# DMA transposes for more tiles, an earlier query block and constant products in front of the value projection

## The reference

```
h = RMSNorm(x) * (1 + scale1) + shift1
q, f, i, g, B, C, hv = h @ W_in                    # 7 blocks of 512 columns
HGRN2 (4 heads of 128): f_t = lb + (1-lb) sigmoid(f);  S_t = diag(f_t) S_{t-1} + (1-f_t) outer i_t
       o_t = S_t^T q_t, RMSNorm per head, times g_onorm * silu(g)
conv:  y = B * causal_conv3(C * hv)
x = x + gate1 * (concat[o, y] @ W_out)
x = x + gate2 * (relu((RMSNorm(x) * (1+scale2) + shift2) @ W_up)^2 @ W_down)
out = RMSNorm(x) * g_final
```

## Time and profile before

| what | value |
|---|---|
| median of 3 runs | 861.19 us (858.78 to 865.7) |
| the profiled execution, its own time | 858.85 us |
| its span on the slowest core (the others: 854.6 to 856.6) | 857.3 us |
| PE busy | 810.3 us, 95% of the span |
| DVE, ACT, POOL busy | 454.1, 369.2, 173.1 us |
| mean granted TensorE clock | 0.991 of full speed |
| HBM traffic | 123.93 MB read, 22.68 MB written |

### The profile page before, as it was taken

One profiled execution on the slowest core, in us unless ns is written; L12 is line 12 of the kernel. 1 busy time (PEld: TensorE's weight loads), 2 busy tenths in 40 slices (PEclk: granted clock), 3 DMA queues, 4 the chain that ended last, 5 costly groups with the idle time before them and its releaser, 6 DMA issues.

```text
span 857.3 us, 16496 instructions; the slowest of 8 cores (854.6 to 857.3 us)
## 1 busy us (share of the span) xinstructions
PE 810.3 (95%) x5917; PEld 512.2 (60%) x5917; DVE 454.1 (53%) x876; ACT 369.2 (43%) x803; POOL 173.1 (20%) x231
## 2 busy tenths in 40 slices
PE   1479999999999999999999999999999999999996
PEld 1348876586876868656545654564456445644864
DVE  2366997377777867953015553455345535541522
ACT  3267963364676778447303322332233213310412
POOL 3110143353324231510003011101110111111002
PEclk9989999999999999999999999999999999999998
DMA  8999935988893349599995325212421432112001
GB/s 151 191 193 189 198 99 95 209 208 175 197 222 129 125 146 153 149 174 192 188 198 184 112 56 160 99 50 62 151 96 50 78 107 75 38 37 99 26 1 50
DMA packets 38957, 109.57 MB, mean 128 GB/s; under 512 B 15030, under 2 KB 16054, under 8 KB 33884
## 3 DMA queue, kind: packets, MB, share of 16 engines
q0 software_dynamic: 6624, 44.14, 31.1%
q1 hardware_dynamic: 30524, 58.34, 22.1%
q10 hardware_dynamic: 1728, 6.03, 2.2%
HBM read 123.93 MB, written 22.68 MB: 171 GB/s over the span
## 4 chain that ended last, share of the span: by engine, by line
PE 83%; DMA 11%; DVE 2%; issue 2%; ACT 1%; POOL 1%; DVEq 0%; ACTq 0%; POOLq 0%; SPq 0%
PE B L510 82%; DMA gates<-xr 4%; DMA win<-w_in 3%; DMA xe<-xp 3%; PE B L521 1%; ACT W L537 1%; DMA xn<-xp 1%; DMA xr<-xs 1%; POOL xr L544 0%; DVE Sd L544 0%; POOL mix L544 0%; DVE W L554 0%; DVE sg L554 0%; DVE ub L544 0%; DVE W L544 0%
## 5 line engine op out<-in xcount | busy, mean ns | idle before, releaser
L510 PE MATMUL B<-h2T,wup 128*128 128x384 bf16 (+1 forms) x1536 | 240.2, 317 | 0.0
L510 PE MATMUL B<-wdn,uT 128*128 128x512 bf16 (+1 forms) x1120 | 235.9, 373 | 0.0
L510 PE MATMUL B<-hT,win 128*128 128x256 bf16 (+1 forms) x1728 | 194.3, 269 | 6.1 <-DMA win<-w_in 5.4
L510 PEld LDWEIGHTS B<-h2T,wup 128*128 128x128 bf16 x1536 | 149.5, 98 | 83.8
L537 ACT ACTIVATE W<-B 128x384 f32<-128x384 f32 (+2 forms) x209 | 103.6, 497 | 204.3 <-PE B L510 187.3
L510 PEld LDWEIGHTS B<-wdn,uT 128*128 128x128 bf16 x1120 | 109.6, 98 | 124.8
L510 PEld LDWEIGHTS B<-hT,win 128*128 128x128 bf16 x1728 | 158.9, 99 | 27.9 <-issue 7.1
L544 POOL TENSOR_TENSOR xr<-xr,W 128x512 f32<-128x512 f32 x63 | 82.3, 1312 | 291.8 <-DVE W L544 256.3
L544 DVE TENSOR_TENSOR uT<-W,B 128x384 bf16<-128x384 f32 (+1 forms) x160 | 83.8, 525 | 80.5 <-ACT W L537 74.8
L544 DVE TENSOR_TENSOR W<-B,Gp 128x512 f32<-128x512 f32 (+1 forms) x65 | 44.2, 680 | 152.9 <-PE B L510 152.7
L537 ACT ACTIVATE W<-xr 128x1024 bf16<-128x1024 f32 (+2 forms) x19 | 18.3, 965 | 131.5 <-POOL xr L544 126.8
(11 more groups left out here) (157 smaller groups left out, 660.9 us busy)
## 6 DMA issues: line engine op xcount, KB each, us to landing
x<-xr SPq DMA_DIRECT2D x17, 512.0 KB, 10.6
xn<-x SPq DMA_DIRECT2D x17, 512.0 KB, 5.8
xr<-x SPq DMA_DIRECT2D x17, 512.0 KB, 4.1
ada<-w_ada POOLq DMA_DIRECT2D x8, 1024.0 KB, 14.7
xr<-xp SPq DMA_DIRECT2D x16, 512.0 KB, 10.0
wup<-w_up POOLq DMA_DIRECT2D x8, 1024.0 KB, 13.7
wdn<-w_down POOLq DMA_DIRECT2D x8, 1024.0 KB, 39.7
yp<-xr SPq DMA_DIRECT2D x15, 512.0 KB, 2.6
```

Of the source, the lines that this page charges most:

```text
L510: ins = e.matmul(o_, lhsT=l_, rhs=r_, start=st, stop=sp_, skip_group_check=True)
```

## The change

Five things change.

1. `sample_mod` no longer transposes on PE. It issues a DMA transpose (`turn`) into its destination and works in place from there. It is used for S in the mixer and in group 1 of the channel mixer.
2. `norm1` takes DMA transposes for P4 to P7: two of them a tile, and eight DVE operations of 256 columns in place.
3. `norm2` takes its `cross` branch for the first two groups too.
4. win0's load is put ahead of P2's `norm1`, and so ahead of the fetch of P2's tokens.
5. Before the first tiles' steps, 14 operations of two matmuls each are recorded: the identity and mask constants times the identity, 384 columns, into a bank of a new class Z. Nothing reads the result. Their priority is the lowest of all, and the planner may start them from 43,000 ns of its clock on.

A DMA's semaphore now goes by the part of the buffer too, so that the two transposes of one tile count apart.

```diff
@@ Prog
-    CAPS = {"G": (2, 4), ...}
+    CAPS = {"Z": (0, 1), "G": (2, 4), ...}
@@ op
+        o.start = 0.0
...
-            key = eng + ((":in:" + writes[0][0].name) if (...) else (":out:" + reads[0][0].name))
+            key = eng + ((":in:" + writes[0][0].name + writes[0][1]) if (...) else (":out:" + reads[0][0].name))
@@ schedule
-            o.est = 0.0
+            o.est = o.start
@@ sample_mod
-        M, Mn = NR.take()
-        Mb = M[:, :].bitcast(BF16)
-        tr([(Mb[:, j * 128:(j + 1) * 128], nbv[:, j * 128:(j + 1) * 128], ident) for j in range(8)], [nbn, "cB"], [Mn])
+        turn(dst[:, :, c0:c0 + 128], nbv, [nbn], [dst_n + "#d0"], 128 * 2048)
...
-            tt("dve", tmv, trv, scb, ALU.mult, [Mn, "modT%d#%d" % (j_sc // 8, jh)], [Wn])
-            tt("dve", hv, tmv, shb, ALU.add, [Wn, "modT%d#%d" % (j_sh // 8, jh)], ["%s#%d" % (dst_n, jh)])
+            tt("dve", tmv, hv, scb, ALU.mult, [dst_n + "#d0", "modT%d#%d" % (j_sc // 8, jh)], [Wn])
+            tt("dve", hv, tmv, shb, ALU.add, [Wn, dst_n + "#d0", "modT%d#%d" % (j_sh // 8, jh)], ["%s#%d" % (dst_n, jh)])
@@ norm1
+        if ti >= 4:
+            for b in range(2):
+                turn(h[:, :, b * 128:(b + 1) * 128], nbs[b][0], [nbs[b][1]], ["%s#d%d" % (hn, b)], 128 * 2048)
+            for jj in range(8):
+                ts("dve", h[:, jj, :], h[:, jj, :], modT[:, 8 + jj, 0:1], modT[:, jj, 0:1], ALU.mult, ALU.add,
+                   [hn + "#d0", hn + "#d1", "modT0#%d" % (jj // 4), "modT1#%d" % (jj // 4)], ["%s#%d" % (hn, jj)])
+            return h, hn
@@ norm2, branch cross
-                turn(dst, nbv, [nbn], [hn], 128 * 2048)
+                turn(dst, nbv, [nbn], [hn + "#d0"], 128 * 2048)
...
-                       ["%s#%d" % (hn, j), "modT2#%d" % (j // 4), "modT3#%d" % (j // 4)], ["%s#%d" % (hn, j)])
+                       [hn + "#d0", "modT2#%d" % (j // 4), "modT3#%d" % (j // 4)], ["%s#%d" % (hn, j)])
@@ the program's order
+    bank, bn = ZB.take()
+    for i in range(14):
+        mm([(bank[:, 0:384], ident, cB[:, 0:384], True, True) for _ in range(2)], ["cB"], [bn], prio=1e6 + i)
+        P.ops[-1].start = 43000.0
...
+    load_in(0)
     hs[2] = norm1(*tiles[2], eng="pool")
-    for j in (0, 3, 5, 6, 4):
+    for j in (3, 5, 6, 4):
         load_in(j)
...
-                norm2(bgroups[0][n_ - 5:n_ - 4], None, "h2T0_", n_ - 5)
+                norm2(bgroups[0][n_ - 5:n_ - 4], None, "h2T0_", n_ - 5, cross=True)
...
-            norm2(bgroups[1], h2T, "h2T", 0, got)
+            norm2(bgroups[1], h2T, "h2T", 0, got, cross=True)
```

More of the change, by code:

```diff
@@ L60 @@
     BANKS = ["B%d" % i for i in range(8)]
-    CAPS = {"G": (2, 4), "M": (1, 2), "N": (0, 1), "U": (2, 3), "O": (1, 2), "D": (0, 1), "P": (0, 2), "X": (0, 8), "Y": (0, 1)}
+    CAPS = {"Z": (0, 1), "G": (2, 4), "M": (1, 2), "N": (0, 1), "U": (2, 3), "O": (1, 2), "D": (0, 1), "P": (0, 2), "X": (0, 8), "Y": (0, 1)}
     FIFO = "PXUN"
@@ L146, in op @@
         if dma is not None:
-            key = eng + ((":in:" + writes[0][0].name) if (writes and (writes[0][0].rng is not None or not reads)) else (":out:" + reads[0][0].name))
+            key = eng + ((":in:" + writes[0][0].name + writes[0][1]) if (writes and (writes[0][0].rng is not None or not reads)) else (":out:" + reads[0][0].name))
             o.chan = key
@@ L740, in take @@
             return PSB[plan[0][k] if plan else "B0"], n
-    GA, MR, NR, UR, OR, DR, PR, GB, YB = (Banks(c) for c in "GMNUODPXY")
+    GA, MR, NR, UR, OR, DR, PR, GB, YB, ZB = (Banks(c) for c in "GMNUODPXYZ")
     MB2 = 1024 * 512 * 4
@@ L879, in sample_mod @@
     def sample_mod(nbv, nbn, dst, dst_n, c0, j_sh, j_sc, spare=None):
-        M, Mn = NR.take()
-        Mb = M[:, :].bitcast(BF16)
-        tr([(Mb[:, j * 128:(j + 1) * 128], nbv[:, j * 128:(j + 1) * 128], ident) for j in range(8)], [nbn, "cB"], [Mn])
+        turn(dst[:, :, c0:c0 + 128], nbv, [nbn], [dst_n + "#d0"], 128 * 2048)
         for jh in range(2):
             W, Wn = (spare[0][:, jh * 512:(jh + 1) * 512], "%s#%d" % (spare[1], jh)) if spare else WT.take()
-            trv = Mb[:, jh * 512:(jh + 1) * 512].rearrange("p (j s t) -> p j s t", s=16, t=8)
             tmv = W[:].rearrange("p (j s t) -> p j s t", s=16, t=8)
```

## The result

The changed kernel takes **894.23 us** (median of 4 runs, 891.59 to 899.69) against 861.8 us for the kernel before on the same chip (median of 4): a ratio of **1.0369, 95% interval 1.0319 to 1.0419**. It is 3.7% slower; the forecast was 853.4 us.

What follows compares the result with a forecast made beforehand. PE's unbroken work after 62.8 us and when it begins bound the kernel; 858.85 - 6.75 (transposes) - 1.0 (start) = 851.1 us, plus 2.34 to the median of runs gives 853.4 us, range 847 to 861.

Steps and rivals of the forecast that it cites:

- So the waits count 0: Mixer and first two channel-mixer groups: DMA transposes land before PE first reads their tokens, so PE's added wait is 0.
- that of DVE's scaling for the landing: The one added wait named for the DMA transposes: DVE's scaling waits for the landing, 3.2 us quiet, 22.5 us taken.
- 22.5 us: Landing time taken for a DMA transpose under load, from SP's transfers between 219 and 257 us.
- the bound of 47 us at one piece a turn: High end for a transpose beside POOL's loads: 64 pieces an engine, 0.73 us a turn, 47 us.
- the 7.75 us forecast: Total gain on PE's path: 6.75 us from transposes leaving PE plus 1.0 us at the start.
- the 11.3 us that I gave P7: Mixer, tile P7: margin from normalised (300.6 us) to first read (311.95 us), without POOL loads; 7.5 us needed.
- The transposes' price: Mixer and first two channel-mixer groups: 15 batches of 8 transposes leave PE at 0.45 us each, 6.75 us gained.
- The start: Before 70 us: win0 ahead of P2's tokens and constant matmuls gain 1.0 us, between 2.9 gained and 2.5 lost.
- Rival A: Mixer: the planner's new order doubles PE's waits or the constants lose 2.5 us, 856 to 859 us; chance 0.20.
- Rival B: Second channel-mixer group: third block waits for a shared normalised buffer, PE stands 18 us, 871 us; chance 0.11.
- Rival C: All 120 moved transposes: each cost PE its duration, 216 ns, so 26 us go and time is 834 us; chance 0.02.
- the 0.66: Whole kernel: chance given to the forecast's own case, 850 to 857 us around 853.4 us.

Runs made afterwards that it cites:

- experiment 12: Changed kernel with P4, P5, the second group and the first group's sample block back on PE, two up-weight loads a tile later, old start: ratio 1.0001 to the kernel before.
- experiment 8: Kernel before with only the changed kernel's start (query block ahead of the tokens, constants), all transposes on PE: ratio 0.9984.
- experiment 4: Kernel before with only the second channel-mixer group's three blocks transposed by DMA: 884.82 us, ratio 1.0305.
- Experiments 5: Changed kernel with P4's transposes back on PE and a third normalise buffer taken from the evacuation's: 903.8 us, ratio 1.0526 to the kernel before.
- experiment 6: Changed kernel with every DMA transpose replaced by a plain copy of the same 1,024 pieces of 256 bytes: 868.9 us, ratio 1.0126 to the kernel before.
- experiment 10: Changed kernel with P4, P5 and the second group back on PE, and the first two up-weight loads a tile later: ratio 1.0045 to the kernel before.

## Why the prediction was wrong

- **The step that failed** is "So the waits count 0". It compared each landing with PE's first read of the transposed tokens and found 34 us for P5 (P4, S and P6 were given the same lead without working it out). I named the added wait, "that of DVE's scaling for the landing", and not what is queued behind it on DVE; and I did not ask who wants the buffer back that the transpose reads. The waits were not 0: ACT stood 24.05 us for the buffer and DVE 28.10 us for the landing, and PE 15.75 us behind them and 11.14 us just before. On core 4 these two deadlines were 219.3 us (DVE, 247.42 - 28.10) and 212.0 us (ACT, 221.84 - 9.80), with another tile's work behind each. I had named the two buffers, but for the second group alone.
- **The landing was mis-sized.** I took 22.5 us for a transpose under load; P4 had 12.4 to 49.6, the second group's first block 62.3 to 68.4. For P4 22.5 us lies within what six of the cores show (12.4 to 31.7), but cores 4 and 7 reached 49.6 and 40.6. For the second group the bound of 47 us at one piece a turn was the better reading, and still too low: 64 pieces an engine in 66 us are 1.03 us a turn, where the plain transfers of the earlier trace rows had 0.73. The Trainium skill, page "DMA: Bandwidth & Descriptors", section "Queues, rings and completion order", gave 3 to 5 us by my estimate from its rule of whole packets; the second group's 62 to 68 us disagree, for transposes and for plain copies of 256 bytes alike.
- **Where no long wait came, the sum was right in direction and too large.** Cores 0 and 3 have spans of 853.8 and 851.8 us, where both took 856.6 before: 2.8 and 4.8 us of the 7.75 us forecast. P6 and P7 landed within 7.2 us, inside the 11.3 us that I gave P7.
- **The transposes' price** of 0.45 us a batch is in PE's work: from the first `up` matmul to `down` core 3 takes 409.13 - 359.47 - 0.99 (a wait) = 48.67 us, where the kernel before took 416.47 - 366.63 = 49.84 us (366.63 is its first `up` matmul in the view of the earlier trace rows): 0.39 us for each of three batches. But PE's sum alone does not set the slowest core's end: experiment 12 shows no gain from seven batches.
- **The start** agrees with the forecast: values in 7.07 us, queries at 58.8 us on core 3 (60.8 in experiment 8; forecast 61), 1.4 us gained of 1.0 forecast, with no gain inside the interval.
- **Rival A** was too small. **Rival B** had its link right in kind, the shared buffer, and its chain wrong: it gave the first and the third block 48.2 us each, and the first took 62.3 to 68.4 us and the third, with the loads through, 7.7 to 10.3. What counts is ACT's order: of the 18 us that it gave PE the changed kernel shows 1.28, experiment 4 25.8. It forecast slower, 871 us; the 894 us came from another place. **Rival C** is out.
- **Two slips in the prediction's sums** change nothing in the account: with the start's 2.9 us gained the case begins at 858.85 - 6.75 - 2.9 + 2.34 = 851.5 us, not 850, and of the 0.66 it gives 0.34 to the side below 852.6 while its words put a little more above.
- That the transposes would slow the loads was in no rival. Experiments 5 and 6 show it; why the engines move half as much while they do is open, beyond that the time goes within the transposes' packets. It happened at 195 to 270 us and not at the mixer's end, where the second group's stretch moved 178 GB/s on core 4 both with transposes and with plain copies.

## What to carry to other kernels

When a transfer takes over an engine's work, ask two things of each place where it will run: what else is in the queues in that very window, and who wants its source buffer back, on which in-order engine, with what behind it. Ask the same of the first instruction that waits for the result. A margin against the last reader says nothing about these two. A transfer that is harmless in the stretch where one can see it (3.2 us) may take twenty times as long in another; move it only into stretches shown to be quiet, and check again after any load is moved, as experiment 10 shows.

## What the runs showed of the hardware that I had not expected

DMA transposes and POOL's loads can jam each other: on core 4 a transpose of 256 KB took 49.6 us and the load beside it 44.2 us, at 99 GB/s in all, where plain copies of the same pieces left 194 GB/s and 11 us. In these traces the late landings had two or more loads beside them. The jam differed between cores that run the same program at the same time (12.4 to 26.9 us for the same transpose).

The issue of a DMA transpose can hold SP for most of the transfer, with all that SP is to issue next. At the second group on core 0 the issues took 14.97 us of a landing of 62.8 and 39.51 us of one of 45.2, against 1.26 us when quiet:

```profile
365.22 14.97 SPq L571 DMA_TRANSPOSE h2T<-W  x1
...
386.92 39.51 SPq L571 DMA_TRANSPOSE h2T<-W  x1
```

The plain copies of experiment 6 held SP for 0.6 and 5.9 to 8.9 us there.
